# A two-stage transformer on one core: the first layer's products from transposed x, with the norm factor applied to their results

## What is computed

```python
h = rmsnorm(x, ln_mix_g)               # x * rsqrt(mean(x*x) + eps) * g, by token
proj = h @ w_in                        # 1024 x 7748
aq, ak, av, iq, ik, iw, hq, hf, hi, hg, cb, cc, ch, gates = split(proj)
q, k = rmsnorm(aq, by head of 64), rmsnorm(ak, by head of 64)
sc = sum over 4 heads of relu(iq . ik) * iw      # the indexer; causal
keep the 64 best keys of each query by sc        # top_k
y_attn = softmax(q . k / 8 + rel_bias) @ v       # 8 heads, over the keys kept
y_hgrn = gated linear recurrence of hq, hf, hi, gated by hg
y_conv = cb * conv3(cc * ch)
x = x + mix(gates, y_attn, y_hgrn, y_conv) @ w_out
x = x + square(relu(rmsnorm(x) @ w_up)) @ w_down
```

## Time and profile before

| | us |
|---|---|
| median of three runs | 1116.42 |
| the profiled execution | 1113.57 |
| its span, first to last instruction | 1111.8 |
| PE busy | 1079.6 (97%) |
| DVE busy | 668.0 (60%) |
| ACT busy | 567.0 (51%) |
| POOL (GpSimd) busy | 10.3 (1%) |
| DMA, mean over the span | 167 GB/s |

### The profile page before, as it was taken

The page is one execution under the profiler, slowest core; times in us unless marked ns, Lnnn a source line. Parts: engine busy times, 40 slices in busy tenths (PEclk is TensorE's granted clock), DMA queues, the critical chain, the costliest instruction groups (busy, mean ns, idle before and its releaser), DMA issues.

```text
span 1111.8 us, 17859 instructions
## 1 busy us (share of the span) xinstructions
PE 1079.6 (97%) x6724; PEld 954.6 (86%) x6724; DVE 668.0 (60%) x968; ACT 567.0 (51%) x802; POOL 10.3 (1%) x15
## 2 busy tenths in 40 slices
PE   6999999999999999999999999999999999999996
PEld 5998877887998899897978999898988779989995
DVE  5797696766655554685546654655744656555543
ACT  6545744755635444544455544544645746444441
POOL 0010010000000000000000000000000000000000
PEclk9999999999999999999999999999999999999998
DMA  7754333555464566464323655565432334556641
GB/s 283 262 175 147 121 120 128 169 197 185 150 225 152 200 214 222 138 227 152 111 81 134 216 196 173 164 207 195 152 133 96 114 107 159 190 200 212 192 132 39
DMA packets 53658, 185.44 MB, mean 167 GB/s; under 512 B 5840, under 2 KB 9184, under 8 KB 53600
## 3 DMA queue, kind: packets, MB, share of 16 engines
q1 hardware_dynamic: 52544, 183.58, 49.4%
q10 hardware_dynamic: 1056, 1.06, 0.3%
HBM read 183.55 MB, written 1.07 MB: 166 GB/s over the span
## 4 chain that ended last, share of the span: by engine, by line
PE 85%; DVE 9%; ACT 3%; DMA 1%; issue 1%; DVEq 0%; SPq 0%; ACTq 0%
PE ps L394 25%; PE ps L396 25%; PE ps L395 25%; DVE wlo L1349 3%; PE ps L463 3%; PE ps L512 2%; PE ps L536 2%; DMA raw<-stream 1%; DVE hT_lo L1369 1%; DVE arena L1458 1%; ACT whi L951 1%; PE ps L587 0%; DVE stat L1457 0%; PE ps L838 0%; PE ps L603 0%
## 5 line engine op out<-in xcount | busy, mean ns | idle before, releaser
L1349 DVE TENSOR_TENSOR wlo<-raw,whi 128x1024 fp32r<-128x1024 f32 x339 | 405.6, 1221 | 193.8 <-ACT whi L951 191.9
L951 ACT ACTIVATE whi<-raw 128x1024 fp32r<-128x1024 f32 x339 | 347.9, 1053 | 187.8 <-PE ps L396 125.9
L394 PE MATMUL ps<-hT_hi,whi 128*128 128x256 f32 x1152 | 328.9, 286 | 0.1
L395 PE MATMUL ps<-hT_lo,whi 128*128 128x256 f32 x1152 | 325.9, 283 | 0.0
L396 PE MATMUL ps<-hT_hi,wlo 128*128 128x256 f32 x1152 | 325.8, 283 | 0.0
L394 PEld LDWEIGHTS ps<-hT_hi,whi 128*128 128x128 f32 x1152 | 220.8, 192 | 2.5 <-DVE hT_lo L1369 1.1
L395 PEld LDWEIGHTS ps<-hT_lo,whi 128*128 128x128 f32 x1152 | 220.9, 192 | 0.7
L396 PEld LDWEIGHTS ps<-hT_hi,wlo 128*128 128x128 f32 x1152 | 220.8, 192 | 0.0
L394 PE MATMUL ps<-whi,y_hi 128*128 128x512 f32 (+1 forms) x540 | 213.6, 395 | 2.6 <-DVE y_lo L1436 2.0
L395 PE MATMUL ps<-wlo,y_hi 128*128 128x512 f32 (+1 forms) x540 | 209.9, 389 | 0.0
L396 PE MATMUL ps<-whi,y_lo 128*128 128x512 f32 (+1 forms) x540 | 209.9, 389 | 0.0
(11 more groups left out here) (209 smaller groups left out, 777.5 us busy)
## 6 DMA issues: line engine op xcount, KB each, us to landing
raw<-stream SPq DMA_DIRECT2D x339, 512.0 KB, 4.3
x<-x_in SPq DMA_DIRECT2D x2, 512.0 KB, 3.8
arena<-scratch ACTq DMA_DIRECT2D x1, 1024.0 KB, 11.6
arena<-rb SPq DMA_DIRECT2D x1, 1024.0 KB, 6.4
bm<-decay SPq DMA_DIRECT2D x1, 1024.0 KB, 8.9
out<-x SPq DMA_DIRECT2D x4, 256.0 KB, 2.1
cst<-const SPq DMA_DIRECT2D x1, 906.0 KB, 9.5
arena<-gfin SPq DMA_DIRECT2D x1, 512.0 KB, 6.4
```

Source lines behind the costliest of these rows:

```text
L394: pe.matmul(o, a[0], b[0], start=start, stop=False)
L395: pe.matmul(o, a[0], b[1], start=False, stop=False)
L951: act.activation(whi[:, u % RING, :], raw[:, u % RAW, :], ACT.Copy).then_inc(sem("hi_done"), 1)
L1349: dve.tensor_tensor(wlo[:, u % RING, :], raw[:, u % RAW, :], whi[:, u % RING, :].bitcast(F32), ALU.subtract).then_inc(sem("lo_done"), 1)
```

## The change

- The order of the first jobs becomes akv, iqk, aq. The indexer's products come at step 7, its scores at step 8, the norms of q and k at steps 10 and 12, their transposes behind unit 15, selection at steps 9, 11 and 13 to 18, the mask at 19, the two parts of bm at 20 and 22.
- A transposed copy of x is a new input. It is loaded in four quarters between the first units. ACT and DVE make hT from it directly with the gain, without the norm factor. x by token is loaded behind unit 15, for the residual alone.
- GpSimd squares the quarters and adds them; PE sums over partitions against a column of ones; the factor's spreading is called in the first layer too. T jobs are multiplied by rs when they are evacuated (two ACT instructions in place of one), iqk by DVE, hf, hq, cc, ch and cb by GpSimd after their evacuation.
- akv's matmuls wait for the quarters of h as they come. Six matmuls on zeros stand ahead.
- The constants are split: the identity, the bias table's one-hot (32 rows), the causal mask, and the rest late. Three that nothing uses are gone. The gains are loaded from ACT's queue.

```diff
-    for name, kind, cols in (("aq", "T", 512), ("akv", "T", 260), ("iqk", "F", 384), ("hf", "F", 512),
+    for name, kind, cols in (("akv", "T", 260), ("iqk", "F", 384), ("aq", "T", 512), ("hf", "F", 512),
...
+            load_x(0)
+            load(0, 0)
+            load_x(1)
+            load_x(2)
+            load(1, 1)
+            load_x(3)
+            load(2, 2)
+            load(3, 3)
+            sp.dma_start(cst[:, 0:C_Z], const[:, 0:C_Z]).then_inc(sem("id_in"), 16)
+            sp.dma_start(cst[0:32, C_OH:N_CONST], const[0:32, C_OH:N_CONST]).then_inc(sem("relb_in"), 16)
             sp.dma_start(stat[0:32, 232:240], relb).then_inc(sem("relb_in"), 16)
+            loads(RAW, 2 * RAW)
+            sp.dma_start(cst[:, C_Z:C_NSUF], const[:, C_Z:C_NSUF]).then_inc(sem("c_in"), 16)
+            loads(2 * RAW, 4 * RAW)
+            for t in range(TT):
+                sp.dma_start(x[:, t, :], x_in[t * P:(t + 1) * P, :]).then_inc(sem("x_in"), 16)
+            sp.dma_start(cst[:, C_NSUF:C_OH], const[:, C_NSUF:C_OH]).then_inc(sem("c_late"), 16)
...
+                            if name == "akv" and t == 0:
+                                pe.wait_ge(sem("n_lo"), kt // 2 + 1)
...
-            pe.wait_ge(sem("id_in"), 32)
-            norm(0)
+            pe.wait_ge(sem("pl_zero"), 1)
+            for _ in range(6):
+                pe.matmul(ps[:, W2, 0:S], hA[:, 0, :], hA.rearrange("p a b -> p (a b)"), start=True, stop=True)
...
+                if u == 2:
+                    pe.wait_ge(sem("ones"), 1)
+                    pe.wait_ge(sem("x_sq"), 1)
+                    for t in range(TT):
+                        for half in range(2):
+                            m = pe.matmul(ps[:, W3, t:t + 1], xsq[:, half * S + t * P:half * S + (t + 1) * P], bias1,
+                                          start=half == 0, stop=half == 1)
+                    m.then_inc(sem("x_ss"), 1)
+                if u == 4:
+                    pe.wait_ge(sem("id_in"), 16)
+                    spread_rs(0)
...
+            act.dma_start(sml[:], small).then_inc(sem("sml_in"), 16)
             act.preload_act_table_set("natural_log_exp_and_others")
+            act.wait_ge(sem("sml_in"), 16)
+            hi_first(0)
+            hi(0)
+            hi_first(1)
+            hi_first(2)
+            hi(1)
+            hi_first(3)
+            for u in range(2, LEAD - 1):
+                hi(u)
+            hi(LEAD - 1)
             rsqrt(rs, nt, "n_v", 1, "n_r")
...
+            for b in range(4):
+                pool.wait_ge(sem(f"xt_in{b}"), 16)
+                c = xT[:, 2 * b:2 * b + 2, :].rearrange("p a b -> p (a b)")
+                pool.tensor_tensor(xsq if b == 0 else xsq2, c, c, ALU.mult).then_inc(sem("pl_link"), 1)
+                pool.wait_ge(sem("pl_link"), 2 + b + max(b - 1, 0))
+                if b:
+                    pool.tensor_tensor(xsq, xsq, xsq2, ALU.add).then_inc(sem("pl_link" if b < 3 else "x_sq"), 1)
+                    if b < 3:
+                        pool.wait_ge(sem("pl_link"), 2 + 2 * b)
+            def by_rs(name, v):
+                pool.wait_ge(sem("evac"), evac_no[name] + 1)
+                pool.tensor_tensor(v, v, rsB[0].unsqueeze(1).to_broadcast([P, 4, S]), ALU.mult).then_inc(sem("by_token"), 1)
...
+            pool.wait_ge(sem("rsB_ok"), 1)
+            by_rs("hf", hz)
+            by_rs("hq", hqf)
+            pool.wait_ge(sem("c_late"), 16)
+            pool.wait_ge(sem("evac"), evac_no["hi"] + 1)
+            spread_inputs(0)
+            by_rs("cc", ccT)
+            by_rs("ch", chT)
+            by_rs("cb", cbT)
...
+            def lo_first(b):
+                dve.wait_ge(sem("n_hi"), b + 1)
+                for k in (2 * b, 2 * b + 1):
+                    m = dve.scalar_tensor_tensor(hT[1][:, k, :], xT[:, k, :], sml[:, G_MIX + k:G_MIX + k + 1],
+                                                 hT[0][:, k, :].bitcast(F32), ALU.mult, ALU.subtract)
+                m.then_inc(sem("n_lo"), 1)
+            dve.memset(bias1, 1.0).then_inc(sem("ones"), 1)
+            lo_first(0)
+            lo(0)
+            lo_first(1)
+            lo_first(2)
+            lo(1)
+            lo_first(3)
+            for u in range(2, LEAD - 1):
+                lo(u)
+            dve.wait_ge(sem("x_ss"), 1)
+            dve.tensor_scalar(nt, ps[:, W3, 0:TT], 1.0 / D, EPS, ALU.mult, ALU.add).then_inc(sem("n_v"), 1)
+            lo(LEAD - 1)
             dve.wait_ge(sem("n_r"), 1)
             refine(rs, nt, tmp2)
+            dve.tensor_scalar(nrs, rs, -1.0, None, ALU.mult).then_inc(sem("n_rs"), 1)
...
+                if u == 5:
+                    keep_rsB(0)
+                if u == 6:
+                    evac_v("iqk", iqk, 1.0, 0)
```

More of the change, by code:

```diff
@@ L93 @@
 JOBS, UNITS = plan()
-C_ID, C_FLIP, C_TRI, C_ONE, C_NSUF, C_NONE, C_Z, C_CM, C_Z2, C_CK, C_ST, C_BD = (P * i for i in range(12))
-C_OH = 12 * P
-C_FREQ = C_OH + 384
+C_ID, C_Z, C_CM, C_NSUF, C_NONE, C_Z2, C_CK, C_ST, C_BD = (P * i for i in range(9))
+C_FREQ = 9 * P
 C_BLK = C_FREQ + 16
-N_CONST = C_BLK + 4
+C_OH = C_BLK + 4
+N_CONST = C_OH + 384
 G_MIX, G_MLP, G_N2, G_M2 = 0, 8, 16, 32
@@ L116, with model @@
 ARENA = 20744
[L119 removed]
+def model(nc, stream, const, small, pos, relb, rb2, gfin, x_in, xt_in, scratch, decay, out):
     with ExitStack() as ctx:
@@ L485, in turn_mixed, with spread_rs @@
                     m.then_inc(sem("mx_tr"), 1)
-            def norm(i):
+            def spread_rs(i):
+                pe.wait_ge(sem("n_rs"), i + 1)
+                pe.wait_ge(sem("n_lo"), 8 * i + 4)
                 for t in range(TT):
[L490 to L496, removed]
-            x_n = arena[:, 0:2048].rearrange("p (a b) -> p a b", a=TT)
+                    m = pe.matmul(ps[:, W3, t * P:(t + 1) * P], rs[:, t:t + 1].to_broadcast([P, P]), cs(C_ID),
+                                  start=True, stop=True)
+                m.then_inc(sem("rsB_ps"), 1)
             def att_logits(a, n, q, k):
@@ L608, in _ @@
             seq = []
-            for name in ("aq", "akv", "iqk", "hf", "hq", "hi", "cc", "ch", "cb", "hg"):
+            for name in ("akv", "iqk", "aq", "hf", "hq", "hi", "cc", "ch", "cb", "hg"):
                 seq += [(name, k, h_all) for k in range(JOBS[name]["n"])]
@@ L637, in _ @@
                     m.then_inc(sem("qk_tr"), 1)
[L638 to L649 removed]
                 if u in steps_a:
                     if u == 23:
[L653 removed]
+                        pe.wait_ge(sem("qk_T"), 1)
                     att_step(0, steps_a[u], dsa_q, dsa_k, dsa_v)
@@ L750, in out_unit @@
                     turn_x(3 if name == "woa" else 5, 1)
-            def spread_rs(i):
-                pe.wait_ge(sem("n_rs"), i)
-                pe.wait_ge(sem("n_lo"), 8 * i + 4)
-                for t in range(TT):
-                    m = pe.matmul(ps[:, W3, t * P:(t + 1) * P], rs[:, t:t + 1].to_broadcast([P, P]), cs(C_ID),
-                                  start=True, stop=True)
-                m.then_inc(sem("rsB_ps"), 1)
             mlp(0)
@@ L1056, in _ @@
                     w = (("bm_ok", 1),) if i == 0 else (("mixed", 2 * i),)
-                    L1[f"g{b}{half}"] = (gate[:, :, half * 512:(half + 1) * 512], ACT.Exp, -1.0, w)
+                    L1[f"g{b}{half}"] = (gate[:, :, half * 512:(half + 1) * 512], ACT.Exp, -1.0, w, 1)
                     no = 2 * i + half
@@ L1070, in _ @@
                     att_step(0, steps_a[u])
+                if u == 4:
+                    evac("akv", kvw, rows=1)
                 hi(u + LEAD)
@@ L1217, in _ @@
                 if u == 17:
-                    evac("bv", bv, rows=1)
+                    evac("bv", bv, rows=2)
                 if base + u in ends and u != 16:
-                    evac(ends[base + u], L2[ends[base + u]], rows=1 if u else None)
+                    evac(ends[base + u], L2[ends[base + u]], rows=2 if u else None)
                 if u == 2:
@@ L1332, in _ @@
                 m.then_inc(sem("hg_i4"), 1)
+            pool.wait_ge(sem("rsB_ok"), 1)
[7 more added lines that the diff above has]
+            by_rs("cb", cbT)
+            for hd in range(1, 4):
+                spread_inputs(hd)
         @block.vector
```

175 lines of the change are left out of this document (78 added, 97 removed).

## The result

The changed kernel takes **1121.74 us** (median of five runs, 1120.51 to 1122.48). The kernel before takes 1115.43 (median of five, 1113.6 to 1116.89). The ratio is 1.0056, interval 1.0041 to 1.0071: **0.56% slower**, some 6.3 us. The profiled execution took 1121.74 for a span of 1119.8. The forecast was +1.5, with a range up to 1120.9: the time lies above it.

What follows compares the result with a forecast made beforehand. PE, busy 97% of the span, was taken to bound the kernel. Head -0.1, PE's added work +1.3, wait at 44 -1.1, wait at 90 +0.2, clock +1.2 make +1.5 us: forecast 1117.9, range 1108.3 to 1120.9.

Steps and rivals of the forecast that it cites:

- The contention is no wall: Faster rival: GpSimd does not hold VectorE off in the head, which gains 5.6; sum -7.5, 1108.9 us, 22%.
- the long ones cost DVE only what overhangs into a subtraction, 1.5 together: Before first attention: GpSimd's products for hf and hq, beside one-input selection, cost VectorE only 1.5 us together.
- The forecast wait of 2.3: Before the first attention step: PE waits about 2.3 us instead of 2.1, so +0.2; bounds 0 to 3.5.
- The clock term: In the head: PE's holes between 5.7 and 15.5 us lower its clock; +1.2 us, between 0 and 1.9.
- the 2.1 us wait did not send it back: At 90 us in the kernel before: PE's wait of 2.1 us did not return the array to its lower speed.
- a gain of 0.1: Head: with GpSimd's squares delaying VectorE, akv ends at 19.0, as if begun at 13.4 instead of 13.5.
- the gain without contention: Head: without GpSimd's contention akv ends at 13.5, as if begun at 7.9, a gain of 5.6 us.
- The covers: ACT's half evacuations lie beside PE, else each late attention step adds 0.3; DMA's constants and late x cost nothing.
- Added work of PE, +1.3: First layer: sums over partitions cost PE 0.8 us (0.5 to 1.2), spreading the norm factor 0.5.
- Wait at 44, -1.1: At 44.1 us: PE's wait for the norm of q and k goes, since their transposes come five units later.
- The slower one: Rival: holes from 5.7 to 15.5 lower the clock, losing 2.6; wait at 90 reaches 3.5; +4.1, 1120.5 us, 24%.
- the two faster rivals: Contention no wall in the head: 1108.9 us, 22%; half of GpSimd's pushes falling where VectorE waits anyway: 1112.7 us, 14%.

Runs made afterwards that it cites:

- products in four: Changed kernel with each of GpSimd's five multiplications by the norm factor cut into four instructions of 128x256: 1119.20 us, ratio 1.0044 to the kernel before.
- without squares: Changed kernel without GpSimd's seven squares and sums in the head, a constant in their place: 1116.21 us, ratio 1.0017 to the kernel before.
- products held back: Changed kernel with GpSimd's work on hf, hq, hi and cc waiting for attention's first to fourth exponential: 1117.36 us, ratio 1.0026 to the kernel before.
- both with 14 warm-ups: The kernel of "both" with 14 instead of 6 matmuls on zeros ahead: 1115.76 us, ratio 1.0014 to the kernel before.
- both: Changed kernel with x loaded behind unit 3, squares on ScalarE instead of GpSimd and PE sums, GpSimd's products waiting for attention's exponentials: 1115.54 us, ratio 1.0012.
- factor on ScalarE and products on VectorE: Changed kernel with squares summed on ScalarE, five products made by VectorE from PSUM, three late things moved up: 1113.61 us, ratio 0.9998 to the kernel before.

## Why the prediction was wrong

**The mechanism held.** PE starved in the head, unit 1 late (forecast 15.5, measured 16.78), PE's wait at 44 gone, a wait of the old kind before attention, DVE stretched beside POOL: all as described. What failed are the sizes: of the 6.5 us between the forecast of +1.5 and the +8.0 of the spans, attention's waits are about 2.4, the head 1.5, small waits 0.6, the clock before attention 0.2 and the stretch at 916, which nothing in the change explains, 1.7. "The contention is no wall" falls. The rule cited from the Trainium skill (SBUF — State Buffer, "Who interferes with whom") agrees with the row at 57.31.

**The step that failed: "the long ones cost DVE only what overhangs into a subtraction, 1.5 together".** They cost 4.4. The argument was that selection reads one input and isn't held off. Selection's instructions are indeed not held off (products in four), but DVE's stretch is a mixture: it reaches an instruction of the kind held off every 2.8 us, and both products met one within 0.1 us of their start. A bound from the rows already cited, the whole length of each, was at hand and was not taken. One input is not what protects an instruction, either: L1549 at 80.45, counted there as one of the two-input kind, reads one, and took 1.20 us where its like takes 0.35 undisturbed (changed kernel, 82.16). The forecast wait of 2.3 had 3.5 as its bound; measured were 4.2, and another 0.6 at 137, where the product of cb held an instruction of two columns for 1.57 us. Against the forecast's +0.2 attention's waits grew by 2.6: +2.4 us.

**The clock term stood in the wrong place.** In the profiled head it did no harm, since unit 1 ran at full speed; in three other kernels with the same head akv ended 2.1 to 3.1 us later; +1.2 was forecast. But behind the longer wait before attention the clock fell for 3.4 us, which no step counted ("the 2.1 us wait did not send it back" was used for a wait that became 4.2). About +1.4 there. That this is near the forecast's 1.2 is luck.

**The head, "a gain of 0.1": a loss of 1.4.** Two terms were mis-sized. x and the first weights landed later than forecast: POOL's row has quarter 0 at 5.03 (forecast 3.5), ACT's rows have unit 0 at 6.28 and unit 1 at 9.01 (4.8 and 7.3). So ACT began its first quarter at 5.14, not 3.9; the gains, which its row names as the last to come, cost only the 0.1 us behind POOL's start. And the gain without contention was not 5.6: without squares akv ended at 16.41, as if begun at 10.8, so 2.7. Of the missing 2.9, PE's work on akv is 1.55: its 48 matmuls take 7.15 us from 9.26 without a pause, instead of 5.6, because the clock is at its lower level until 12.2. The other 1.35 are the later start. GpSimd took 4.05, where 5.5 were forecast; so the head's number missed by less than its two terms.

**Added work of PE, +1.3:** 0.81 for the sums and 0.54 for the spreading, as forecast. **Wait at 44, -1.1:** right. **Small waits, +0.6:** not foreseen; two of 0.3 each, at the indexer and before the transposes of q and k. **The covers** named for ACT's halves and DMA held in the changed kernel; in the runs where x came early, the DMA's did not.

**The rivals.** The slower one came near in its number (1120.5 against 1121.7) and had half of the cause: the wait before attention, which went past its bound, but half speed in unit 1 only in other kernels with this head (akv at 22.6 to 23.6). Its sum has 2.6 for the clock in the head and no term for the head's late start: that the two nearly make up for each other is luck. In the chances, the two faster rivals and a tenth of the forecast make 0.40, not 0.38; nothing rests on it.

## What to carry to other kernels

Before work goes to GpSimd because it is idle, ask whether VectorE is full in that stretch. Here the first four of GpSimd's five products (2.4 to 2.9 us) cost VectorE 2.2 each and the fifth 1.4, however small the instruction that they met, and cutting them up saved little; only selection's instructions lost nothing beside one. Cost it at full length, and give it to whoever already reads the result from PSUM, or put it where VectorE waits. And of a change that lengthens a wait, cost the clock behind the wait as well.

## What the runs showed of the hardware

- A DVE instruction of 128x20 took 2.39 us beside a POOL product, 0.18 without; one of 128x2 took 1.55 against 0.17; a multiplication by a constant, of one SBUF input, took 2.90 where it usually takes 0.69. So it isn't only the two-input kind that is held off, as the prediction assumed. Selection's instructions (0.27 to 0.43 us, run with products in four) and the maximum of the logits with its mask, read from PSUM and SBUF (0.41 us at 112.75, products held back), kept their lengths beside a POOL product.
- The same head ran at different clocks: akv ended at 20.46 and 20.64 in two kernels, at 22.56, 22.67 and 23.56 in three others with the same instructions up to there.
- The length of a wait alone does not tell whether the clock falls: it fell behind waits of 1.3 (at 116, products held back, and both with 14 warm-ups), 2.4 (the indexer's, with 14 warm-ups), 2.7, 2.8 and 4.2 to 4.4 us, and stayed up behind 1.3 (at 113, both), 2.1 (before), 2.4 and 2.5 (the indexer's, with 6 warm-ups) and 2.8 (before attention, factor on ScalarE and products on VectorE):

```profile
80.00:90.00 10.00, 7.19 (x57) 6.62 (x56) 8.04 (x11) 2.76 (x6) 0.07 (x1) 1.00 0.63 209
```

What sets it is open; no run here varied it by itself. Open too is why it fell at 916 in one execution of the changed kernel, far behind anything that the change touches.

- The kernel before has such differences too. Its 79 executions beside the experiments took 1113.3 us on average at a granted clock (mean over the span) of 0.997 or 0.998, 1114.6 at 0.996 and 1116.0 at 0.994. The five of the changed kernel had 0.988 to 0.991.
